# Attention with two heads on separate rows of TensorE, and a second staging buffer for the context's weights

## The chip, the cores and the metric

The kernel runs on one core of one Trainium2 chip. The metric is the device time of one execution in microseconds (us). TensorE (PE in the rows) multiplies and turns, VectorE is DVE, ScalarE is ACT, GpSimd is POOL, and SyncE (SP) issues the transfers. Each engine takes its own instructions strictly in order; semaphores order them against each other.

## The reference, cut to what matters

Two transformer blocks on 1024 tokens of width 1024, in fp32. The change touches the first block from its start up to the merge of the two attentions, and nothing of the feed-forward layers or of the second block.

```python
h  = modulate(rms_norm(x,   g1), sh1, sc1)     # 1024 tokens
hc = modulate(rms_norm(ctx, g1), csh1, csc1)   # 256 context tokens
q_a,k_a,v_a,q_b,k_b,v_b = split(h @ w_in)      # heads of 64; 8 query heads, 2 key heads in a
k_ac,v_ac,k_bc,v_bc     = split(hc @ w_in)     # the queries of the context are not needed
q, k = rms_norm per head; q_a, k_a = rope(...)
# A: blocks of 128 queries, keys of the block and its two neighbours, and the context
p = softmax([q_a k_a^T * 1/8 | band mask, q_a k_ac^T * 1/8, sink]);  o_a = p [v_a; v_ac]
# B: 128 queries (2 rows of a 16x64 grid), keys of 8 or 9 grid rows, and the context
p = softmax([q_b k_b^T * 1/8 + bias | mask, q_b k_bc^T * 1/8]);      o_b = p [v_b; v_bc]
x = x + g * concat(rms_norm(o_a), rms_norm(o_b)) @ w_out    # then SwiGLU, then block 2
```

## The kernel before, in words

A product of fp32 matrices is made of three products of the fast format fp32r: each operand is split into a high part and the rest (`w_hi`, `w_lo`, `ht_hi`, `ht_lo`), and high x high, high x rest and rest x high are added up.

**Context stage.** The 2 context tiles and then the 8 tiles of x are normed (`sum_tile` on ScalarE, `norm_tile` on GpSimd), scaled on VectorE (`scale_tile`, L278), shifted on GpSimd (`shift_tile`, L283), turned on TensorE (`turn_tile`, L293), and split on their way out of PSUM by ScalarE (`turned_hi`, L304) and VectorE (`turned_lo`, L308). Beside it go 5 panels of `w_in` (256 columns each) for the context: one buffer `stage` takes a panel, `split_hi` (ScalarE, L359) and `split_lo` (VectorE, L363) split it into one of two slots, and `load_weights` fetches the next panel when the split of the last is done. The loops of `pe_c`, `act_c`, `dve_c` and `pool_c` take one panel and one tile of x in each step: 5 steps with a panel, 3 with a tile alone. Then 9 panels for x follow, 8 tiles each.

**Keys.** Each of 10 token tiles holds 10 key heads. A key is split first (`key_hi`, `keys_dve`, L580), high part and rest side by side, then turned (100 turns), and copied to `kt`, so that a turned key head fills 128 rows: 64 of high parts, 64 of rests. `pool_q` does the same for each query tile of two heads, once as high|rest and once as rest|high; `pe_turn_q` turns these four.

**Attention.** A unit is one pair of heads (i = 0 to 3) and one block of 128 queries (n = 0 to 7); 32 units of phase A, then 32 of phase B. For each head j of the pair: scores (`pe_scores`, L744, two products on all 128 rows per piece of keys), mask and row minimum (`dve_min`, L925; the scores carry a minus), exponential and sum (`act_exp`, L841, L844, L846), turns of the probabilities (`pe_turn_p`, L754 the first four pieces, L761 the rest), copies to `prob_t` (`dve_p`, L932, 4 pieces; `act_p`, L857, the rest), products with the values of both heads on separate columns (`pe_values`, L775), and out (`dve_o`, `pe_turn_o`, L781, `dve_on`, L961). `act_v` copies the values of the pair to `v_pair` once per pair, and waits for all products of the last pair. In units with n = 0, 1, 6, 7 of phase B, which are called edge units here, `dve_min` and `act_exp` work in two steps each, the second step of the exponential reading the masked scores; the other units are joined. `dve_tables` makes the tables of bias of a pair. Between A and B everything runs empty, and then B's first queries are turned.

The order in a unit is written out by hand. TensorE's is

```python
pe_turn_p(n, 0); pe_scores(n+1, 0); pe_values(n-1); pe_turn_q(n+2)
pe_turn_p(n, 1); pe_scores(n+1, 1); pe_turn_o(n-1)
```

After attention all engines meet at a barrier; whatever comes after it is not touched, but for one instruction per tile in the merge.

## Time and profile before

| | |
|---|---|
| median of 3 runs | 2659.41 us (2658.87 to 2660.73) |
| the profiled execution's own time | 2660.4 us |
| its span | 2658.6 us |
| mean granted clock of TensorE | 0.965 |
| busy TensorE / VectorE / ScalarE / GpSimd | 92% / 61% / 40% / 13% of the span |
| 44.0 to 123.4 us | context stage |
| 123.4 to 361.6 us | 9 panels for x |
| 361.6 to 378.2 us | keys |
| 378.2 to 529.6 us | attention, phase A |
| 529.6 to 739.3 us | attention, phase B, and the barrier |
| 739.3 us to the end | merge, feed-forward, second block |

The span runs from the first to the last instruction; the execution's own time has 1.8 us around it. An engine's busy share says nothing of what limits a stage: a stage is as long as the chain of waits through it. The stretches are read from the first product of each stage, and the time between two equal instructions of neighbouring units is the period of the loop.

### The profile page before, as it was taken

The numbers are of one execution on the slowest core, as the hardware profiler recorded it, in microseconds if no ns is written. First come the engines' busy times: TensorE is split into PE (matmuls) and PEld (weight loads), VectorE is DVE, ScalarE is ACT, GpSimd is POOL, SyncE is SP. The second block draws the span as 40 slices with busy tenths as digits, with TensorE's granted clock in tenths as the row PEclk, the third lists the DMA queues.
The fourth block names the chain that finished last, engine by engine and source line by source line (L and its number), as shares of the span: only waits on it lengthen the run. The fifth ranks groups of instructions, "written<-read, shape, count | busy, mean of one in ns | idle before, by whom it ended". The sixth has DMA issues, their size and how long they took to land. (4 is left out here: it accounts for less than half of the span.)

```text
span 2658.6 us, 42198 instructions
## 1 busy us (share of the span) xinstructions
PE 2458.3 (92%) x15597; PEld 2118.0 (80%) x15597; DVE 1618.2 (61%) x2691; ACT 1064.3 (40%) x2111; POOL 358.6 (13%) x507
## 2 busy tenths in 40 slices
PE   4799989989869799999999999997897999999998
PEld 2788887778769688888888799995795888878886
DVE  3523347767755877777677932107538777667677
ACT  1422245555531432333254432224435454544444
POOL 2566312222111100000000010003212000000001
PEclk8899999999979899999999999997998999999999
DMA  8233320000042133233375431110231444377453
GB/s 290 92 115 113 124 54 1 1 2 1 1 151 80 64 104 103 91 119 103 109 263 184 141 116 48 39 36 3 75 109 64 156 155 148 135 254 252 135 186 115
DMA packets 189033, 288.15 MB, mean 108 GB/s; under 512 B 11704, under 2 KB 109948, under 8 KB 188540
## 3 DMA queue, kind: packets, MB, share of 16 engines
q1 hardware_dynamic: 188860, 285.84, 32.2%
q8 instruction: 109, 1.79, 0.3%
q14 instruction: 64, 0.52, 0.1%
HBM read 219.46 MB, written 67.34 MB: 108 GB/s over the span
## 5 line engine op out<-in xcount | busy, mean ns | idle before, releaser
L378 PE MATMUL ps<-w_hi,ht_hi 128*128 128x256 f32 x1744 | 504.0, 289 | 17.6 <-DVE w_lo L363 8.3
L379 PE MATMUL ps<-w_lo,ht_hi 128*128 128x256 f32 x1744 | 498.4, 286 | 0.0
L380 PE MATMUL ps<-w_hi,ht_lo 128*128 128x256 f32 x1744 | 498.0, 286 | 0.0
L378 PEld LDWEIGHTS ps<-w_hi,ht_hi 128*128 128x128 f32 x1744 | 338.1, 194 | 34.3 <-issue 11.3
L379 PEld LDWEIGHTS ps<-w_lo,ht_hi 128*128 128x128 f32 x1744 | 338.3, 194 | 0.0
L380 PEld LDWEIGHTS ps<-w_hi,ht_lo 128*128 128x128 f32 x1744 | 338.1, 194 | 0.0
L363 DVE TENSOR_TENSOR w_lo<-stage,w_hi 128x2048 fp32r<-128x2048 f32 x31 | 73.9, 2382 | 217.5 <-ACT w_hi L359 217.5
L1687 PE MATMUL ps<-ff_b_hi,ff_a_hi 128*128 128x512 f32 x448 | 174.6, 390 | 2.6 <-DVE ff_b_lo L1675 1.4
L1689 PE MATMUL ps<-ff_b_hi,ff_a_lo 128*128 128x512 f32 x448 | 174.3, 389 | 0.0
L1688 PE MATMUL ps<-ff_b_lo,ff_a_hi 128*128 128x512 f32 x448 | 174.3, 389 | 0.0
L1445 PE MATMUL ps<-ht_hi,swiglu_w_hi 128*128 128x512 f32 x352 | 138.2, 393 | 10.1 <-DVE tmp L1955 7.7
L1402 ACT ACTIVATE swiglu_w_hi<-swiglu_stage 128x512 fp32r<-128x512 f32 x110 | 69.0, 631 | 175.1 <-PE ps L1447 153.2
L1446 PE MATMUL ps<-ht_lo,swiglu_w_hi 128*128 128x512 f32 x352 | 137.6, 391 | 0.0
L1447 PE MATMUL ps<-ht_hi,swiglu_w_lo 128*128 128x512 f32 x352 | 137.5, 391 | 0.0
L1648 ACT ACTIVATE ff_a_hi<-ff_a_raw 128x512 fp32r<-128x512 f32 x112 | 70.8, 632 | 165.7 <-PE ps L1689 148.7
L1673 DVE TENSOR_TENSOR ff_a_lo<-ff_a_raw,ff_a_hi 128x512 fp32r<-128x512 f32 x112 | 77.5, 692 | 90.0 <-ACT ff_a_hi L1648 89.9
L1687 PE MATMUL ps<-swiglu_b_hi,swiglu_a_hi 128*128 128x512 f32 x308 | 120.5, 391 | 5.0 <-DVE swiglu_b_lo L1675 5.0
L1689 PE MATMUL ps<-swiglu_b_hi,swiglu_a_lo 128*128 128x512 f32 x308 | 119.9, 389 | 0.0
L1688 PE MATMUL ps<-swiglu_b_lo,swiglu_a_hi 128*128 128x512 f32 x308 | 119.9, 389 | 0.0
L775 PE MATMUL ps<-prob_t,v_pair 128*64 128x128 f32 (+1 forms) x1440 | 96.1, 279 | 23.9 <-ACT v_pair L869 9.0
L841 ACT ACTIVATE probs<-masked,small 128x641 f32<-128x641 f32 (+2 forms) x96 | 83.1, 866 | 83.6 <-DVE small L925 83.5
L744 PE MATMUL ps<-kt,q_t 128*128 (+3 forms) x640 | 115.8, 312 | 0.0
(362 smaller groups left out, 5731.7 us busy)
## 6 DMA issues: line engine op xcount, KB each, us to landing
ff_a_raw<-ff_act_dram SPq DMA_DIRECT2D x112, 256.0 KB, 2.8
stage<-w_in SPq DMA_DIRECT2D x23, 1024.0 KB, 5.2
swiglu_a_raw<-swiglu_act_dram SPq DMA_DIRECT2D x77, 256.0 KB, 3.2
stage<-w_mod SPq DMA_DIRECT2D x16, 1024.0 KB, 5.5
ff_stage<-w_ff SPq DMA_DIRECT2D x16, 1024.0 KB, 5.4
ff_act_dram<-ff_act_sums SPq DMA_DIRECT2D x16, 1024.0 KB, 4.3
ff_act_dram<-ff_acts SPq DMA_DIRECT2D x16, 768.0 KB, 5.7
swiglu_stage<-w_up SPq DMA_DIRECT2D x11, 1024.0 KB, 5.2
```

The costliest lines, as they stand in the source:

```text
L378: pe.matmul(bank, a, wh[:, k, :], start=(k == 0), stop=False)
L379: pe.matmul(bank, a, wl[:, k, :], start=False, stop=False)
L380: mm = pe.matmul(bank, b, wh[:, k, :], start=False, stop=(k == KT - 1))
L744: mm = pe.matmul(dst, q_t[:, n % 2, j, o, :], keys_of(ph, i, j, a, w), start=(o == 0), stop=(o == 1))
L775: mm = pe.matmul(ps[HD * j:HD * j + HD, 7, 0:P], v_pair[0:rows, tile, HD * j:HD * j + HD], prob_t[n % 2][0:rows, j, c * P:(c + 1) * P], st ...
L841: act.activation(probs_s[:, j, first:8 + CTX + width], masked_s[:, j, first:8 + CTX + width], ACT.Exp, bias=low, scale=-1.0, accum_out=den ...
L1445: pe.matmul(bank(q, b), w7_hi[b][:, k, :], x_of(0, b, k), start=(k == 0), stop=False)
L1446: pe.matmul(bank(q, b), w7_hi[b][:, k, :], x_of(1, b, k), start=False, stop=False)
L1447: mm = pe.matmul(bank(q, b), w7_lo[b][:, k, :], x_of(0, b, k), start=False, stop=(k == 3))
L1687: pe.matmul(bank, a_hi[r][:, cols], b_hi[r][:, :], start=first, stop=False)
L1688: pe.matmul(bank, a_hi[r][:, cols], b_lo[r][:, :], start=False, stop=False)
L1689: return pe.matmul(bank, a_lo[r][:, cols], b_hi[r][:, :], start=False, stop=last)
```

## The change

- Context: a second buffer `stage_2` takes the panels 1, 3 and 5, the first of them fetched in the middle of the tiles of x. VectorE shifts the two context tiles itself and makes the gain of x after them. All 8 tiles of x are spread over the 5 steps with a panel (`TURNS`), two in a step or one, and turned between the row tiles of a panel.
- Keys and queries are turned unsplit (50 turns for the keys, one per query block and pair, four at a time), and split when they leave PSUM: ScalarE takes the high part, VectorE the rest. `kt` holds two heads on 2 x 64 rows, high parts and rests apart. `k_split`, `q_split`, `v_pair`, `pool_q` and `act_v` are gone.
- Scores: three products per piece and head on 64 rows, the two heads in turn on rows 0 to 63 and 64 to 127. The head pairs of phase A are (i, i+4), one of each key head, for which the query columns are stored in another order, undone in the merge by one more instruction per tile.
- Scores of the next unit come first in a unit, both heads together; all pieces of a head's probabilities leave PSUM in one copy, head 0 by ScalarE, head 1 by VectorE. The first scores of B follow A's last unit without a break, and the tables are made in four parts.

The diff, with its core alone; the lines taken out are those of the functions printed above.

```diff
+    stage_2 = at("stage_2", [2048], F32, nat + NT * D * 4 + 10 * KVW * 4 + 12288)
...
+    kt = at("kt", [5, 2, S + CTX], F32R, ht)
...
         def load_weights(sp, p, source, dst=None):
+            if isinstance(p, int) and p in SECOND:
+                if p > 1:
+                    sp.wait_ge(w_lo_done, p - 1)
+                sp.dma_start(stage_2[:, :].rearrange("p (k n) -> p k n", k=KT), source).then_inc(w_landed_2, 16)
+                return
+            if isinstance(p, int) and p - 1 in SECOND:
+                sp.wait_ge(w_lo_done, p - 1)
+            elif not isinstance(p, int) or p > 0:
                 sp.wait_ge(w_lo_done, p)
             sp.dma_start(stage_up() if dst is None else dst, source).then_inc(w_landed, 16)
...
+        SECOND = (1, 3, 5)
...
         def keys_pe(pe):
+            pe_turn_q(pe, 0, 0, 0)
             pe.wait_ge(dense_evac, D_O)
+            pe.wait_ge(modx_row, 16)
             for j in range(10):
+                if j >= 3:
+                    pe.wait_ge(kt_lo, j - 2)
+                for h in range(5):
+                    col = A_KV + P * h if h < 4 else 0
+                    mm = pe.transpose(ps[:, 2 * (j % 3) + h // 4, (h % 4) * P:(h % 4 + 1) * P], k_nat[:, j, col:col + P], ident[:, :])
                 mm.then_inc(kt_tr, 1)
...
         def keys_act(act):
...
+            act.wait_ge(*panel_used(P_O - 1))
+            act_q(act, 0, 0, 0)
             for j in range(10):
                 act.wait_ge(kt_tr, j + 1)
...
+                act.activation(kt[:, :, 0, j * P:(j + 1) * P], turned_keys(j), ACT.Copy).then_inc(kt_hi, 1)
...
         def keys_dve(dve):
...
+            dve_q(dve, 0, 0, 0)
...
             for j in range(10):
...
+                dve.wait_ge(kt_hi, j + 1)
+                dve.tensor_tensor(kt[:, :, 1, j * P:(j + 1) * P], turned_keys(j), kt[:, :, 0, j * P:(j + 1) * P].bitcast(F32),
+                                  ALU.subtract).then_inc(kt_lo, 1)
...
+        TURNS = [(0, 1), (2, 3), (4,), (5,), (6, 7)]
...
+            for s, turns in enumerate(TURNS):
+                for j in turns:
+                    if j + 2 < NT:
+                        norm_tile(pool, j + 2, T_X, D)
+                        shift_tile(pool, j + 2, NC, shift_x)
...
         def pe_c(pe):
...
+            for s, turns in enumerate(TURNS):
+                for b in rows_pe(pe, s, s % 2, NC, T_C, NC * s, lag=2, at=C_AT):
+                    if b < len(turns):
+                        turn_tile(pe, turns[b], turns[b] % 2, T_X)
...
+            for s, turns in enumerate(TURNS):
+                split_hi(act, s + 1, (s + 1) % 2)
+                if s < 4:
+                    turn(turns[0])
+                heads_act(act, C_PANELS[s], None, NC, NT, NC * s, NC * s)
+                for j in turns[1 if s < 4 else 0:]:
+                    turn(j)
...
+            def turn(j):
+                turned_lo(dve, j, j % 2, T_X)
+                x_scaled(j + 2)
...
+            for s, turns in enumerate(TURNS):
+                if s < 4:
+                    turn(turns[0])
+                heads_dve(dve, C_PANELS[s], last, s + 1, NC, NT, NC * s, NC * s, n)
+                last, n = (C_PANELS[s], n + 1) if C_PANELS[s][0] != "v" else (None, n)
+                for j in turns[1 if s < 4 else 0:]:
+                    turn(j)
...
+            rows = slice(HD * j, HD * j + HD)
...
+                return kt[rows, 4, part, a:a + width]
+            if isinstance(i, int):
+                return kt[rows, i, part, a:a + width]
+            return kt[rows, ds(i, 1), part, a:a + width].squeeze(1)
...
...
+                pe.wait_ge(ql_done, g)
+            for b in range(4):
+                mm = pe.transpose(ps[:, 6, b * P:(b + 1) * P], pair_cols(ph, i, n + b), ident[:, :])
             mm.then_inc(qt_done, 1)
...
+        def pe_scores(pe, ph, i, n):
...
+            pe.wait_ge(ql_done, quad(ph, i, n) + 1)
+            if isinstance(u, int) and u == 0:
+                pe.wait_ge(kt_hi, 10)
+                pe.wait_ge(kt_lo, 10)
+            elif joined(*preceding(ph, i, n)[0::2]):
+                pe.wait_ge(min_done, 2 * u)
+            else:
+                pe.wait_ge(exp_done, 2 * u)
+            if ph == A:
+                parts = [(0, CTX, S, CTX), (1, 0, first * P, width)]
+            else:
+                parts = [(0, 0, S, CTX), (0, CTX, first * P, 256), (1, 0, first * P + 256, width - 256)]
+            for bank, at0, a, w in parts:
+                for m, (x, y) in enumerate(((0, 0), (0, 1), (1, 0))):
+                    for j in range(2):
+                        mm = pe.matmul(ps[:, 2 * j + bank, at0:at0 + w], q_t[HD * j:HD * j + HD, n // 4, x, (n % 4) * P:(n % 4 + 1) * P],
+                                       keys_of(ph, i, j, y, a, w), start=(m == 0), stop=(m == 2))
+            mm.then_inc(s_done, 1)
...
+            if j:
+                pe.wait_ge(pa_evac, u + 1)
+            elif not isinstance(u, int) or u > 0:
+                pe.wait_ge(pb_evac, u)
...
         def attention_pe(pe):
+            pe_scores(pe, A, 0, 0)
...
+                def pair(i, ph=ph):
                     for n in range(NB):
+                        ahead, behind = following(ph, i, n), preceding(ph, i, n)
+                        if ahead:
+                            pe_scores(pe, *ahead)
                         pe_turn_p(pe, ph, i, n, 0)
                         if behind:
+                            pe_values(pe, *behind)
+                        if n % 4 == 1 and next_quad(ph, i, n):
+                            pe_turn_q(pe, *next_quad(ph, i, n))
                         pe_turn_p(pe, ph, i, n, 1)
                         if behind:
...
+        def act_p(act, ph, i, n):
             u = unit(ph, i, n)
+            act.wait_ge(pt_done, 2 * u + 1)
             if not isinstance(u, int) or u > 1:
...
+            act.activation(prob_t[n % 2][:, 0, 0:cols], source, ACT.Copy).then_inc(pa_evac, 1)
...
                     for n in range(NB):
+                        ahead = following(ph, i, n)
+                        act_p(act, ph, i, n)
                         for j in range(2):
...
+                        if n % 4 == 1 and next_quad(ph, i, n):
+                            act_q(act, *next_quad(ph, i, n))
...
+        def dve_q(dve, ph, i, n):
+            dve.wait_ge(qh_done, quad(ph, i, n) + 1)
+            dve.tensor_tensor(q_t[:, n // 4, 1, :], ps[:, 6, :], q_t[:, n // 4, 0, :].bitcast(F32), ALU.subtract).then_inc(ql_done, 1)
...
+            dve.wait_ge(s_done, u + 1)
+            if not isinstance(u, int) or u > 0:
+                dve.wait_ge(exp_done, 2 * u - 1 + j)
...
+            dve.wait_ge(pt_done, 2 * u + 2)
...
+            dve.tensor_copy(prob_t[n % 2][:, 1, 0:cols], source).then_inc(pb_evac, 1)
...
+            dve.memset(inner[:, :, 0:CTX], 0.0)
...
+                        ahead, behind = following(ph, i, n), preceding(ph, i, n)
                         if ahead:
+                            dve_min(dve, *ahead, 0)
+                            dve_min(dve, *ahead, 1)
                         if behind:
...
+                            dve_o(dve, *behind)
                         dve_sums(dve, ph, i, n)
...
+                        dve_p(dve, ph, i, n)
+                        if n % 4 == 2 and next_quad(ph, i, n):
+                            dve_q(dve, *next_quad(ph, i, n))
                         if behind:
...
+                            dve_on(dve, *behind)
+                        if following(ph, i, NB - 1) and (ph == B or isinstance(i, int) and i == PAIRS - 1):
+                            heads = 0 if ph == A else i + 1
+                            if n == NB - 2:
+                                dve_edge(dve, heads, 0)
+                                dve_edge(dve, heads, 1)
+                            if n == NB - 1:
+                                dve_inner(dve, heads, 0)
+                        if ph == B and n == 0:
+                            dve_inner(dve, i, 1)
...
                 sp.dma_start(q_nat[:, j, :], t["x"][0, j * P:(j + 1) * P, :]).then_inc(x_in[j], 16)
+                if j == 3:
+                    load_weights(sp, 1, panel_of(t["w_in"], CTX_COLS[1]))
...
+            dve.wait_ge(mod_added, 16)
+            dve.scalar_tensor_tensor(out=gain_c, in0=gain_c, scalar=1.0, in1=norm1[:, :], op0=ALU.add, op1=ALU.mult).then_inc(mod_added, 1)
+            for j in range(NC):
+                if j == 0:
+                    dve.wait_ge(mod_added, 17)
+                scale_tile(dve, j, j, T_C, ctx_in[:, j, :], gain_c, True)
+                dve.wait_ge(xs_done, j + 1)
+                dve.tensor_tensor(xn[:, j, :], xn[:, j, :], shift_c, ALU.add).then_inc(xn_done, 1)
+            dve.scalar_tensor_tensor(out=gain_x, in0=gain_x, scalar=1.0, in1=norm1[:, :], op0=ALU.add, op1=ALU.mult).then_inc(mod_added, 1)
+            split_lo(dve, 0, 0)
+            for j in range(NC):
+                turned_lo(dve, j, j, T_C, at=C_AT)
...
+            dve_c(dve)
...
+                    source, gain, dst = row_tile(q_nat, j, g * AW, AW), on_ab[:, g * AW:(g + 1) * AW], xn[:, b, g * AW:(g + 1) * AW]
+                    if g == 1:
+                        last = dve.scalar_tensor_tensor(out=dst, in0=source, scalar=root, in1=gain, op0=ALU.mult, op1=ALU.mult)
+                        continue
+                    for kv in range(2):
+                        dve.scalar_tensor_tensor(out=dst[:, kv * PN:(kv + 1) * PN].rearrange("p (i d) -> p i d", d=HD),
+                                                 in0=source.rearrange("p (i j d) -> p i j d", j=2, d=HD)[:, :, kv, :], scalar=root,
+                                                 in1=gain[:, kv * PN:(kv + 1) * PN].rearrange("p (i d) -> p i d", d=HD),
+                                                 op0=ALU.mult, op1=ALU.mult)
```

TensorE in the middle of phase A, one unit from one turn of probabilities to the same turn of the next; L744 are scores, L775 values, L721 the query's turns. Before:

```order
913 L754 MATMUL ps<-ident,probs 128x128 x4
914 L761 MATMUL ps<-ident,probs 128x128
915 L744 MATMUL ps<-kt,q_t 128x256 x2
916 L744 MATMUL ps<-kt,q_t 128x384 x2
917 L775 MATMUL ps<-prob_t_90,v_pair 64x128 x10
918 L721 MATMUL ps<-ident,q_split 128x128 x4
919 L754 MATMUL ps<-ident,probs 128x128 x4
920 L761 MATMUL ps<-ident,probs 128x128
921 L744 MATMUL ps<-kt,q_t 128x256 x2
922 L744 MATMUL ps<-kt,q_t 128x384 x2
923 L781 MATMUL ps<-ident,o_t 128x128
```

The same place in the changed kernel; L769 are scores, L781 probabilities, L794 values, L800 the output's turn.

```order
946 L769 MATMUL ps<-kt,q_t 128x256 x6
947 L769 MATMUL ps<-kt,q_t 128x384 x6
948 L781 MATMUL ps<-ident,probs 128x128 x5
949 L794 MATMUL ps<-prob_t_91,v_nat 64x128 x10
950 L781 MATMUL ps<-ident,probs 128x128 x5
951 L800 MATMUL ps<-ident,o_t 128x128
```

The scores stand ahead of everything else in the unit, 12 products in place of 8; the query's four turns are left in two units of eight only.

VectorE in the context stage from the gain of the context to the second panel's split; L278 scales, L308 splits a turned tile, L363 a panel. Before:

```order
18 L1178 SCALAR_TENSOR_TENSOR mod_83<-mod_83,norm_84 128x1024 x2
19 L278 SCALAR_TENSOR_TENSOR xn<-ctx_in,rstd,mod_83 128x1024 x2
20 L308 TENSOR_TENSOR ht_lo<-ps,ht_hi 128x8x128 x2
21 L363 TENSOR_TENSOR w_lo<-stage,w_hi 128x2048
22 L1184 TENSOR_SCALAR head_gain<-head_gain 128x64 x2
23 L1185 TENSOR_SCALAR neg_sink<-neg_sink 128x8
24 L278 SCALAR_TENSOR_TENSOR xn<-q_nat,rstd,mod_83 128x1024
25 L363 TENSOR_TENSOR w_lo<-stage,w_hi 128x2048
```

In the changed kernel, where L294, L324 and L379 are the same three and L1154 is the shift:

```order
19 L294 SCALAR_TENSOR_TENSOR xn<-ctx_in,rstd,mod_84 128x1024
20 L1154 TENSOR_TENSOR xn<-xn,mod_84 128x1024
21 L294 SCALAR_TENSOR_TENSOR xn<-ctx_in,rstd,mod_84 128x1024
22 L1154 TENSOR_TENSOR xn<-xn,mod_84 128x1024
23 L1155 SCALAR_TENSOR_TENSOR mod_84<-mod_84,norm_85 128x1024
24 L379 TENSOR_TENSOR w_lo<-stage,w_hi 128x2048
25 L324 TENSOR_TENSOR ht_lo<-ps,ht_hi 128x8x128 x2
26 L294 SCALAR_TENSOR_TENSOR xn<-q_nat,rstd,mod_84 128x1024 x2
27 L324 TENSOR_TENSOR ht_lo<-ps,ht_hi 128x8x128
28 L294 SCALAR_TENSOR_TENSOR xn<-q_nat,rstd,mod_84 128x1024
29 L379 TENSOR_TENSOR w_lo<-stage_69,w_hi 128x2048
```

The split of the first panel moved ahead of the turned context tiles, and three tiles of x are scaled ahead of the second panel's split, where one was.

## Rows read from the trace of the kernel before

**Rows 1.** Stretches: engine busy us (count), PEclk granted clock, DMA share, GB/s.
```profile
44.00:123.40 79.40, 51.15 (x320) 47.81 (x321) 46.60 (x41) 33.27 (x49) 46.97 (x35) 0.73 0.38 129
123.40:361.60 238.20, 238.20 (x2018) 216.34 (x2016) 69.90 (x107) 60.13 (x147) 108.09 (x57) 1.00 0.32 106
361.60:378.20 16.60, 13.28 (x110) 11.68 (x109) 11.95 (x17) 13.54 (x29) 4.04 (x12) 1.00 0.33 81
378.20:529.60 151.40, 136.20 (x1326) 114.54 (x1324) 113.06 (x337) 87.53 (x217) 40.24 (x126) 1.00 0.05 9
529.60:739.30 209.70, 178.96 (x1788) 160.68 (x1788) 145.01 (x369) 118.69 (x292) 42.48 (x120) 0.96 0.01 1
```

**Rows 2.** Timeline of the context stage: start, us, engine, line, operation, idle before.
```profile
44.63 2.36 DVE L1178 SCALAR_TENSOR_TENSOR mod<-mod,norm 128x1024 f32<-128x1024 f32 x2
...
65.75 1.91 ACT L359 ACTIVATE w_hi<-stage 128x2048 fp32r<-128x2048 f32 x1 [6.32 <-DMA stage<-w_in]
67.70 2.29 DVE L363 TENSOR_TENSOR w_lo<-stage,w_hi 128x2048 fp32r<-128x2048 f32 x1 [5.37 <-ACT w_hi L359]
...
70.32 1.27 DVE L278 SCALAR_TENSOR_TENSOR xn<-q_nat,rstd,mod 128x1024 f32<-128x1024 f32 x1
72.07 1.23 DVE L308 TENSOR_TENSOR ht_lo<-ps,ht_hi 128x1024 fp32r<-128x1024 f32 x1 [0.47 <-ACT ht_hi L304]
...
96.56 3.80 DVE L363 TENSOR_TENSOR w_lo<-stage,w_hi 128x2048 fp32r<-128x2048 f32 x1 [3.49 <-ACT w_hi L359]
...
123.43 0.56 PE L378 MATMUL ps<-w_hi,ht_hi 128*128 128x256 f32 x1
```

**Rows 3.** The page's DMA issues: count, KB each, us from issue to landing.
```profile
stage<-w_in SPq DMA_DIRECT2D x23, 1024.0 KB, 5.2
```

**Rows 4.** Timeline of VectorE while the keys are turned.
```profile
366.44 0.81 DVE L580 TENSOR_TENSOR k_split<-k_nat,k_split 128x640 f32<-128x640 f32 x1
```

**Rows 5.** Timeline of TensorE, one phase-A unit.
```profile
441.83 1.31 PE L775 MATMUL ps<-prob_t,v_pair 128*64 128x128 f32 x20
443.08 0.66 PE L721 MATMUL ps<-ident,q_split 128*128 128x128 f32 x4
443.57 0.60 PE L754 MATMUL ps<-ident,probs 128*128 128x128 f32 x4
444.01 0.27 PE L761 MATMUL ps<-ident,probs 128*128 128x128 f32 x1
444.03 0.83 PE L744 MATMUL ps<-kt,q_t 128*128 x4
```

**Rows 6.** The same timeline, ScalarE and VectorE.
```profile
443.04 0.83 ACT L841 ACTIVATE probs<-masked,small 128x641 f32<-128x641 f32 x1 [0.59 <-DVE small L925]
...
444.21 0.69 DVE L932 COPY prob_t<-ps 128x512 f32<-128x512 f32 x1 [0.72 <-PE ps L754]
444.91 0.88 DVE L925 CUSTOM_DVE_ANT_0 masked<-ps,band,small 128x640 f32<-128x640 f32 x1
```

**Rows 7.** Timeline of VectorE, last row sum of A and first of B.
```profile
526.62 0.15 DVE L947 RECIPROCAL rden<-den 128x2 f32<-128x2 f32 x1
...
543.50 0.17 DVE L947 RECIPROCAL rden<-dsum 128x2 f32<-128x2 f32 x1
```

**Rows 8.** Groups by form in phase B: count | busy, mean ns | idle before.
```profile
L775 PE MATMUL ps<-prob_t,v_pair 128*64 128x128 f32 x768 | 50.0, 279 | 15.2 <-ACT v_pair L869 9.0 <-DVE q_nat L961 6.1
...
L920 DVE TENSOR_REDUCE small<-ps 128x1 f32<-128x256 f32 x32 | 13.4, 420 | 5.0 <-PE ps L744 4.9
...
L925 DVE CUSTOM_DVE_ANT_0 masked<-ps,edge,small 128x512 f32<-128x512 f32 x32 | 24.0, 751 | 4.1 <-issue 0.5
...
L844 ACT ACTIVATE probs<-ps,small 128x256 f32<-128x256 f32 x32 | 15.2, 475 | 44.2 <-DVE small L925 44.2
...
L846 ACT ACTIVATE probs<-masked,small 128x512 f32<-128x512 f32 x32 | 22.8, 711 | 0.0
...
L973 DVE SCALAR_TENSOR_TENSOR edge<-raw_bias,col_mask 128x896 f32<-128x896 f32 x8 | 8.4, 1090 | 0.0
```

414 lines of the change are left out of this document (125 added, 289 removed).

## The prediction, made blind

> **What bounds the kernel now.** I read the stretches first, with the granted clock [rows 1]; then the timelines of the four places that the change touches, on all engines; then the groups by form, for what a wait costs in total. The nine panels for x are TensorE's own: 238.20 us busy of 238.20, 2018 products, so 0.118 us for one of 256 columns. Nothing in the change touches that rate, so this stretch only moves, and so does everything behind the barrier. The other four stretches have air in them: TensorE is busy 51 of 79 us in the context stage, at a mean clock of 0.73; 13.3 of 16.6 at the keys; 136 of 151 in phase A and 179 of 210 in B. These 457 us are what can shrink. All sums are against the profiled execution's own 2660.4 us; the median of the runs shown is 1.0 below it, which I take off at the end.
>
> **Context stage.** The reader is to see one loop [rows 2, 3]: a panel lands 5.2 us after its issue, its high part takes ScalarE 1.91 and its rest VectorE 2.29, and only then is the next one fetched. So a step costs 9.4 us or more whatever it holds, five of them stand in a row, and three tiles of x are left behind them until the first product for x at 123.43. With the second buffer a panel is fetched one step earlier and its 5.2 us lie beside the step before. What is late next is VectorE's row of work. The start: gain of the context 1.18 (half of 2.36) from 44.63, two scalings at 1.27 and two shifts (1.2 each, an estimate by the scaling of the same size) done on VectorE itself, the gain of x 1.18, the first rest 2.29, two turned context tiles at 1.23: done at 56.7. A step with two tiles of x then holds one rest, two scalings, two turned rests and about 1.1 of head sums, 8.4 us, and around 1.6 of waiting for TensorE in between, 10 us. The step's first turned tile waits for its turn behind 24 products (2.8 us), and the panel's rest is queued behind it on VectorE, so TensorE's next panel waits for both. Second panel from 68.7, then 78.7, 88.7 and 98.7, the last two tiles turned at 107; first product for x at about 108, **-15.5 us**. From one side, VectorE's work alone adds up to 48 us behind 44.6, which would be -30. From the other, one of the rests took 3.80 in place of 2.29 while GpSimd worked beside it, and there is more such company now: four times 1.5 us leaves -9. The panel fetched in the middle of x's tiles delays tiles 4 to 7 and the small constants by up to 5 us; tile 4 is needed at about 71, the constants after 107. GpSimd loses two shifts and is not late.
>
> **Keys.** Before, 16.6 us from the last panel to the first score [rows 1]. Now a tile takes five turns (0.11 each, below), a high part of 640 columns on ScalarE and a rest of 640 columns on VectorE; the same work from SBUF took 0.81 [rows 4]. Ten rests in a row behind 0.5 of waiting, 0.55 of turns, 0.25 to their end and about 0.7 of high part are 10.1 us: **-6.5 us**, give or take 1.5. The first query's turn and split lie ahead of it. The gains and the rope are done well before.
>
> **Attention, phase A.** First the prices on TensorE [rows 5]. Turns of 128 columns step by 0.11 (four of them from 443.57 to 444.01). The 20 recorded value products end 1.31 after the first began; less one product's 0.27 that is 1.04, 0.055 each, half a turn's step: products for separate columns of the array ran two at a time. Leaving them costs 0.10 more than a step: the last began at 442.87, the next turn at 443.08. I take this 0.10 for each change of the array's shape. A score of 384 columns is 1.5 times 0.118, 0.177. By this rule an inner unit before is 8 scores 1.18, 10 turns 1.10, values 1.10, four turns of the query 0.44, output 0.11, two changes 0.20: 4.13 us, where 151.4 / 32 = 4.73 were needed; the rest is waiting.
> After: six pairs of scores 3 x (0.118 + 0.177) = 0.885 if the two heads run side by side on their rows, 1.10, 1.10, 0.11 for a quarter of a query's turns, 0.11, and four changes 0.40: 3.71. Units at the band's ends (two of eight) have 4 pieces: 3.09. Waits: the scores of n+1 stand at the head of TensorE's queue and need both minima of n; behind them stand the turns of n and the values of n-1, and ScalarE's copy waits for those turns. From the end of one unit's scores, VectorE needs 0.2 + 2 x 0.88 [rows 6] to the second minimum, 2.0 us, and TensorE comes for it after 2.8: met. VectorE's copy (640 columns, about 0.83 by the 0.69 for 512) ends some 0.1 before TensorE wants the place again: just met. So TensorE is the bound, with 0.15 per unit for such near misses: 6 x 3.71 + 2 x 3.09 + 1.2 = 29.6 per pair, 118.4 for four. ScalarE has two exponentials (0.83 and about 0.1), one copy and a quarter of a query, 2.9 of 3.7. What else goes: the copy of the values to `v_pair` and the wait for it, GpSimd's four operations per unit, which nothing waited for (0).
>
> **The seam and phase B.** From the last row sum of A to the first of B are 16.88 us [rows 7]; now one unit and the tables, about 7. In B a joined unit is scores 3 x (0.118 + 0.118 + 0.147) = 1.15, turns 1.54, values 1.54, 0.22, five changes 0.50: 4.95. The four edge units are a chain instead, since the next scores now wait for both exponentials: scores 1.06, change and turns 0.76, values and changes 1.52, turns 0.66, 0.27 to the end of the last, exponentials 1.19 [rows 8], a start of 0.1: 5.5. The minima (2 x (0.42 + 0.75)) lie beside it. One query in each pair stands in such a chain, 0.44, and VectorE's two tables of 1.09 stick out by about 1.5. Pair: 4 x 4.95 + 4 x 5.5 + 0.44 + 1.5 = 43.7. Before, the values alone waited 9.0 us for `v_pair` in B [rows 8].
> From the first score to the merge: 3.3 until the first turn, 118.4, 1.5 for B's first tables, 174.8 for B less 3.0 for what its last unit lacks, 5 for the end and the barrier: 300, against 151.4 + 209.7 = 361.1: **-61 us**.
>
> **Merge.** Eight more VectorE instructions, two of 256 columns for one of 512; 2 x 0.42 against 0.69 [rows 6, 8] is 0.15 each, half of it hidden: +0.6.
>
> Sum: 2660.4 - 15.5 - 6.5 - 61.1 + 0.6 = 2577.9, as a median **2577 us**.
>
> **What is not in the trace: two heads on separate rows.** No row shows two products on rows 0 to 63 and 64 to 127. Best end: as the columns do, a pair in the time of one product, taken above. Below nothing is excluded, since the columns to stream are the same. Worst end: one after the other, each paying the change of shape. I take the best end, since the value products are the nearest row: same array, two parts, alternating.
> The Trainium skill (TensorE: Matmul & The Clock Gate, LDWEIGHTS) says that a load of weights takes the time of its columns, however few rows it has. That speaks against the change, which makes 12 loads of 128 columns out of 8; by it a pair could be no faster than two loads. The same page (Part 3: Packing small matmuls) says that loads for different rows overlap, with which the sum stays. No run here shows either.
>
> **Rivals.**
> *Loads in a row.* A load of 128 columns and its turn step by 0.11; if the loads of both heads share one way in, a unit's scores take 12 x 0.11 = 1.32 (+0.44, at the band's ends +0.61), in B 18 x 0.11 = 1.98 (+0.83, edge units +0.92): 24 x 0.44 + 8 x 0.61 + 16 x 0.83 + 16 x 0.92 = 43.5 us, 2620. The value products don't tell: the loads of a pair there are 64 columns each, 128 together, and a pair steps by 0.11.
> *Heads in a row.* The scores take twice: 24 x 0.885 + 8 x 0.71 + 16 x 1.15 + 16 x 1.06 = 62 us, 2639.
> *The order eats it.* The two places that are only just met in A are missed: turns wait for VectorE's copy, its copy for the turns, and a unit takes 4.2 in place of 3.7 and half a microsecond more in B too: 64 x 0.5 = 32 us, 2609. For it: 0.6 of waiting per unit before.
> *Slower.* Each step from one group of rows to the other is a change of shape that empties the array: 12 x (0.148 + 0.10) = 2.97 for the scores of an inner unit (+2.1), 1.9 more at the band's ends, +2.95 and +2.86 in B: 24 x 2.09 + 8 x 1.9 + 16 x 2.95 + 16 x 2.86 = 158 us, 2735. It turns the sign from 82 / 64 = 1.3 us per unit on. Against it: value products alternate between columns without any such price.
>
> **Chances.** Forecast 0.60 (own range 2560 to 2592), the order 0.12, loads 0.14, heads 0.09, slower 0.05. The range 2556 to 2630 holds the first three and the bounds of the context. No change within 0.2% (5 us, what a measurement of this kernel can tell) would need two of these to meet by accident: 0.01. Faster 0.94, slower 0.05.
>
> **What would show it.** First product for x at 108 (99 to 114); 10 us from the last panel to the first score; two score products starting within 0.02 us and the next pair 0.118 or 0.177 later; period 3.7 in A and 4.95 and 5.5 in B; one unit at the seam. I am wrong if score products step by 0.11 or more within a pair, if TensorE stands before L781 or L769 for over 0.3 us in each unit of A, or if the panels' rests in the context come no closer than 11 us.

## The result: 36 us faster, less than half of what was forecast

The changed kernel takes 2624.16 us (median of 4, 2621.37 to 2627.89), the one before 2660.07 in the same session: a ratio of 0.9864 (95% interval 0.9852 to 0.9876). The forecast was 2577, so of 83 us there came 36. The range of 2556 to 2630 holds the time, but the reasons behind its middle did not hold, and the range had been drawn for other losses than those that came.

The profiled execution has a span of 2622.9 us. Its stretches, as in [rows 1] (first product for x, last panel, first score, first merge transfer as bounds):

```profile
44.00:118.00 74.00, 49.06 (x324) 46.57 (x322) 52.55 (x39) 32.72 (x49) 38.73 (x30) 0.82 0.40 137
118.00:355.40 237.40, 237.40 (x2017) 215.70 (x2018) 68.56 (x108) 58.38 (x145) 113.37 (x60) 1.00 0.33 106
355.40:365.80 10.40, 7.67 (x58) 5.71 (x56) 8.47 (x12) 8.79 (x13) 0.00 (x0) 1.00 0.22 61
365.79:699.47 333.68, 285.90 (x3244) 232.80 (x3244) 240.22 (x656) 183.02 (x400) 0.00 (x0) 0.98 0.04 7
```

The same last stretch of the kernel before:

```profile
378.17:739.31 361.14, 315.19 (x3115) 275.24 (x3113) 258.07 (x705) 206.23 (x508) 82.76 (x245) 0.98 0.02 4
```

| | before | after | change | forecast |
|---|---|---|---|---|
| first product for x | 123.43 | 117.97 | -5.5 | -15.5 |
| from there to the first score | 254.7 | 247.8 | -6.9 | -6.5 |
| first score to merge | 361.1 | 333.7 | -27.5 | -61 |
| merge to the end | 1919.3 | 1923.4 | +4.1 | +0.6 |

These are single profiled executions. Six of the kernels below hold the context stage of the changed kernel line by line, and their first product for x comes at 114.88 to 120.24; with the old context stage it comes at 123.43 and, in experiment 7, at 125.33. So the context's gain is 3 to 10 us, by which two executions are compared, and -5.5 is one such pair. Part of the spread is TensorE's clock: from the first product of the last panel to the first product for x are 9.32 us in the changed kernel, at a mean granted clock of 0.82, and 7.81 in experiment 5, at 1.00.

The reader is to see in the last two windows that TensorE's busy time fell by 29 us, and that it stands as long as before: 46 us then, 48 now. The waits have moved. They stand on the page, in front of the context's first products (L394) and of the scores (L769):

```profile
L394 PE MATMUL ps<-w_hi,ht_hi 128*128 128x256 f32 x1744 | 506.0, 290 | 28.6 <-DVE w_lo L379 17.2
L769 PE MATMUL ps<-kt,q_t 64*128 64x256 f32 (+2 forms) x960 | 81.1, 307 | 40.6 <-DVE q_t L886 22.6
```

L886 (`dve_q`) makes the rest of the queries; most of what is left of the 40.6 us are B's edge units, whose scores wait for exponentials (14.0 us). The timeline around one such wait, in phase A:

```profile
414.48 0.58 ACT L837 ACTIVATE q_t<-ps 128x512 fp32r<-128x512 f32 x1
...
416.60 0.53 PEld L781 LDWEIGHTS ps<-ident,probs 128*128 128x128 f32 x5 [0.17 <-issue]
...
417.41 0.82 DVE L929 COPY prob_t<-ps 128x640 f32<-128x640 f32 x1 [0.32 <-PE ps L781]
...
418.15 0.68 DVE L886 TENSOR_TENSOR q_t<-ps,q_t 128x512 fp32r<-128x512 f32 x1
...
418.89 1.15 PE L769 MATMUL ps<-kt,q_t 64*128 64x256 f32 x12 [1.40 <-DVE q_t L886]
```

The high part was ready at 415.1. Its rest stands on VectorE behind the copy L929 of the unit, which waits for turns that TensorE has just done; TensorE comes to the next quad's scores at once, and waits for copy and rest: 1.40 us, and 1.67 in B, at one unit in four (a new quad, four blocks of queries turned together). A clean unit beside it takes 3.82 us from row sum to row sum (3.86 forecast), the one with the wait 5.29.

In the context the loop has the same shape. VectorE and GpSimd, and TensorE's first product of a panel:

```profile
58.70 2.37 POOL L299 TENSOR_TENSOR xn<-xn,mod 128x1024 f32<-128x1024 f32 x1
58.76 3.39 DVE L294 SCALAR_TENSOR_TENSOR xn<-q_nat,rstd,mod 128x1024 f32<-128x1024 f32 x1 [0.43 <-POOL rstd L279]
...
65.58 1.28 DVE L294 SCALAR_TENSOR_TENSOR xn<-q_nat,rstd,mod 128x1024 f32<-128x1024 f32 x1 [0.93 <-POOL rstd L279]
...
66.79 2.28 DVE L379 TENSOR_TENSOR w_lo<-stage,w_hi 128x2048 fp32r<-128x2048 f32 x1
66.95 4.39 POOL L299 TENSOR_TENSOR xn<-xn,mod 128x1024 f32<-128x1024 f32 x1 [1.40 <-DVE xn L294]
...
69.13 0.39 PE L394 MATMUL ps<-w_hi,ht_hi 128*128 128x256 f32 x1 [3.10 <-DVE w_lo L379]
...
96.33 0.58 PE L394 MATMUL ps<-w_hi,ht_hi 128*128 128x256 f32 x1 [6.24 <-DVE w_lo L379]
```

The panel's high part was ready at 58.8. Its rest L379 comes 8 us later, behind a scaling that waits for a root from GpSimd. And GpSimd's shift L299 takes 2.37 us where it comes first, and 4.39 where that rest has begun before it.

### The profile page after: what moved, and what is told of

It is laid out like the page before. It is cut to its first block and busy times, and to the rows that moved or that the text cites. A ratio compares the mean times of both kernels' runs of the same rounds, so it can differ in the third digit from the quotient of the medians.

```text
span 2622.9 us, 41034 instructions
## 1 busy us (share of the span) xinstructions
PE 2426.6 (93%) x15675; PEld 2075.1 (79%) x15675; DVE 1601.9 (61%) x2643; ACT 1033.2 (39%) x1983; POOL 268.3 (10%) x249
## 5 line engine op out<-in xcount | busy, mean ns | idle before, releaser
L394 PE MATMUL ps<-w_hi,ht_hi 128*128 128x256 f32 x1744 | 506.0, 290 | 28.6 <-DVE w_lo L379 17.2
L394 PEld LDWEIGHTS ps<-w_hi,ht_hi 128*128 128x128 f32 x1744 | 339.4, 195 | 45.5 <-DVE w_lo L379 18.5
L379 DVE TENSOR_TENSOR w_lo<-stage,w_hi 128x2048 fp32r<-128x2048 f32 x31 | 71.4, 2303 | 197.8 <-ACT w_hi L375 197.8
L275 POOL TENSOR_SCALAR msq<-sumsq 128x1 f32<-128x1 f32 (+1 forms) x26 | 8.1, 310 | 1088.8 <-ACT junk L287 703.4
L769 PE MATMUL ps<-kt,q_t 64*128 64x256 f32 (+2 forms) x960 | 81.1, 307 | 40.6 <-DVE q_t L886 22.6
L1423 PE MATMUL ps<-ht_hi,ff_w_hi 128*128 128x512 f32 x256 | 101.0, 395 | 10.7 <-DVE ht_lo L1324 8.9
```

Source lines behind the costliest of these rows:

```text
L379: dve.tensor_tensor(w_lo[:, slot, :], staged(p)[:, :], w_hi[:, slot, :].bitcast(F32), ALU.subtract).then_inc(w_lo_done, 1)
L394: pe.matmul(bank, a, wh[:, k, :], start=(k == 0), stop=False)
L769: mm = pe.matmul(ps[:, 2 * j + bank, at0:at0 + w], q_t[HD * j:HD * j + HD, n // 4, x, (n % 4) * P:(n % 4 + 1) * P], keys_of(ph, i, j, y, a ...
L1423: pe.matmul(bank(q, b), w7_hi[b][:, k, :], x_of(0, b, k), start=(k == 0), stop=False)
```

## The experiments

Each ratio is against the kernel before in the same session; "attention" is from the first score to the merge, in the profiled run. With the attention of the changed kernel unaltered it took 333.7 to 337.5 us (the changed kernel and experiments 8, 9 and 10), which is how closely these can be compared.

**1. The query's rest ahead of the copy** (`k1`) and **2. the high part between the exponentials as well** (`k7`).

```diff
                         dve_sums(dve, ph, i, n)
+                        if n % 4 == 2 and next_quad(ph, i, n):
+                            dve_q(dve, *next_quad(ph, i, n))
                         dve_p(dve, ph, i, n)
-                        if n % 4 == 2 and next_quad(ph, i, n):
-                            dve_q(dve, *next_quad(ph, i, n))
# k7 also, in attention_act:
                         for j in range(2):
                             if ahead:
                                 act_exp(act, *ahead, j)
-                        if n % 4 == 1 and next_quad(ph, i, n):
-                            act_q(act, *next_quad(ph, i, n))
+                            if j == 0 and n % 4 == 1 and next_quad(ph, i, n):
+                                act_q(act, *next_quad(ph, i, n))
```

> The changed kernel with one move on VectorE: in the third unit of each quad the query's rest stands ahead of the unit's copy of the turned probabilities, where it stood behind it. Theory 1 (the score products of the next quad stand at the head of TensorE's queue and wait for this rest): in the trace of the changed kernel they stood 1.40 us in A and 1.67 in B, 16 places, 22.6 us in all. The rest takes 0.68 and fills 0.32 us in which VectorE waited for the turns, so the copy comes 0.36 later; the wait falls from 1.4 to about 0.4 and the units' periods of 5.29 and 5.44 go to about 4.4: 13 to 18 us faster, 2607 to 2611. Theory 2 (VectorE's row of work sets these units, whatever the order): the copy is later by what the scores gain, and the time stays at 2624.

> As the first kernel of this call, and ScalarE's high part of the query stands between the two exponentials of its unit instead of behind both. Theory 1: this high part was ready 3.1 us before VectorE took its rest, so it is not late, and moving it changes nothing beside the first kernel; in phase A it falls into 0.7 us in which ScalarE waits for turns (0 to -2 us), in B's edge units, where the exponentials free the banks of the next scores, it costs up to 0.58 for each of 8 places (+2 to +5). Theory 2 (the high part on ScalarE is what is late): the time falls by 5 us or more beside the first kernel.

Measured: 2612.27 (ratio 0.9817, 0.9802 to 0.9831), attention 321.4, the unit of 5.29 now 4.19; and 2614.39 (0.9811, 0.9796 to 0.9825), attention 321.3. The wait was the rest's place on VectorE; where ScalarE makes the high part makes no difference that these runs can tell. The times lie a little above the 2607 to 2611 that were expected.

**3. Both halves where their engines are idle** (`k2`): the high part as in `k7`, and `dve_q` at the end of the unit with n % 4 == 1, behind `dve_on`.

> The changed kernel with both halves of the query's split moved to where their engines stand idle: ScalarE's high part between its two exponentials, VectorE's rest at the end of the quad's second unit, behind the scaling of the output, one unit earlier than in the changed kernel. Theory 1 (the next quad's scores waited for the rest; what was left with the rest ahead of the copy, 0.37 us per place, is the later copy of the probabilities): the minima that now come 0.4 us later have slack of 0.7, the units before a new quad go from 5.29 (4.19 with the first remedy) to 3.8 or 3.9 in A and from 6.86 (5.26) to 5.1 in B, first score to merge 313 to 317 us where it was 333.7 and 321.4: 17 to 20 us faster than the changed kernel, 2604 to 2608. Theory 2 (any place on VectorE costs the same 0.4, VectorE being as full as TensorE in these units): 321 us and 2611 to 2614 again.

Measured: 2608.64 (0.9792, 0.9775 to 0.9808), attention 316.9, units before a new quad 3.80 in A and 5.12 in B. So the wait had cost 333.7 - 316.9 = 16.8 us (15.7 to 20.5 over all pairs of runs with these two attentions); the remaining 0.37 per place was the late copy. The page had 22.6 us of waiting for the rest: 5 of them turned into waiting for B's exponentials, which went from 14.0 to 19.0. The window of this kernel, TensorE busy in the second place:

```profile
368.07:685.00 316.93, 287.43 (x3244) 234.88 (x3244) 238.84 (x656) 185.16 (x400) 0.00 (x0) 0.97 0.04 8
```

The work is that of the changed kernel; the waiting fell from 48 to 29.5 us.

**4. The second head on the first one's rows** (`s10`).

```diff
-  q_t[HD * j:HD * j + HD, n // 4, x, ...], keys_of(ph, i, j, y, a, w)
+  q_t[0:HD, n // 4, x, ...],               keys_of(ph, i, 0, y, a, w)
```

> The changed kernel, in which the score products of the second head read rows 0 to 63 too (it computes the first head's scores twice; the second head's are left out). As many instructions, columns and waits. Theory 1 (separate rows let two products run at once): with one group of rows they stand in a row, 0.885 us more per unit of A, 0.71 at the band's ends, 1.15 and 1.06 in B; TensorE is the bound in A, so a clean unit goes from 3.82 to 4.7: first score to merge +62 us, 2675 to 2690. Theory 2 (the pairs only start together in the records, and the array was never shared): clean units stay at 3.8 and the time at 2621 to 2628.

Measured: 2720.17 (1.0207, 1.0184 to 1.0231). The twelve score products of an inner unit of A, in this kernel and then in the changed one:

```profile
442.84 2.05 PE L769 MATMUL ps<-kt,q_t 64*128 64x256 f32 x12
```

```profile
422.70 1.15 PE L769 MATMUL ps<-kt,q_t 64*128 64x256 f32 x12
```

0.90 more, where the rows of before gave 0.885, and the clean unit went from 3.82 to 4.70. There no two products start together: they step by 0.117 to 0.121, and by 0.174 to 0.185 with 384 columns. Separate rows do run two products in the time of one. The time came out 30 us above the range of Theory 1. Beyond its 62 us there are 55 more in the window of the profiled run:

```profile
363.02:813.50 450.48, 403.58 (x3244) 342.92 (x3244) 241.46 (x656) 182.67 (x400) 0.00 (x0) 0.85 0.03 5
```

The mean granted clock fell to 0.85, with TensorE busier than before (90% of the stretch against 86%). This profiled run took 2737.18 us, 17 above the median of the five, at a mean clock over the span of 0.945 where the others had 0.950 to 0.953; so at the median some 38 of the 55 us are left. Which property of the work lowers the clock is not settled, nor how much of the 55 us is the clock's.

**5. Head by head** (`k5`): `for j` outside, `for m` inside in the score loop.

> The changed kernel with one loop turned: the three score products of the first head stand ahead of the three of the second, so that neighbours in TensorE's queue are on the same rows of the array and only one pair of six overlaps. Theory 1 (two heads run at once on separate rows, which is what halves the scores): a part of two pairs lost of three costs 2 x 0.118 or 0.177: 0.6 us per inner unit of A, 0.5 at the ends, 0.77 in B: 24 x 0.6 + 8 x 0.5 + 32 x 0.75 = 42 us if TensorE is the bound everywhere, less a part in the edge units and where scores wait: 25 to 42 us slower than the changed kernel, 2650 to 2666. Theory 2 (the two heads' products only start together in the records; the array takes them one after the other anyway): no change, 2621 to 2628.

Measured: 2630.5 (0.9879, 0.9860 to 0.9897), its interval meets that of the changed kernel; clean units 3.83. Theory 2 gave the right number, but experiment 4 refutes its reason. The start times in the trace suggest why: 419.681 and 419.691, 419.905 and 419.917, 420.021 and 420.038. Products still start in pairs, and the twelve take 1.15 us as in the changed kernel, where twelve on one group of rows took 2.05. So the pairs should be of the two heads, although three of one head stand ahead of three of the other in the program. That is inferred: a record names neither its rows nor its head.

**6. The order undone** (`k6`) and **7. the order alone, in the kernel before** (`s11`).

```diff
# k6, the changed kernel; s11 does the reverse in the kernel before, for both heads
+                        pe_turn_p(pe, ph, i, n, 0)
                         if ahead:
                             pe_scores(pe, *ahead)
-                        pe_turn_p(pe, ph, i, n, 0)
# s11 also: dve_min of both heads ahead of the unit's dve_p; in joined units
+                    pe.wait_ge(min_done, 2 * u - 1 + j)     # was exp_done
```

> The changed kernel with one part of the order undone: the next unit's scores stand behind the turns of the first head's probabilities, as before, and no longer at the head of the unit. Theory 1 (in A TensorE is busy throughout a clean unit of 3.82 us, so that its order is worth nothing there; at the 16 places where the scores wait for the query's rest, the turns of 0.77 us fill the wait): clean units stay at 3.8, the places with a wait go from 5.29 to 4.5 or 4.6; in B's edge units the scores come 0.8 later and the chain through the exponentials pays for it in 16 units: -12 + 8, so 2615 to 2628. Theory 2 (scores first is what keeps VectorE and ScalarE fed): clean units of A go to 4.4 or more as before the change, and the time rises by 20 us or more, 2644 and up.

> The kernel before with the new order alone: both heads' next scores at the head of TensorE's unit, VectorE's minima ahead of its copies, and in joined units the scores wait for the minimum and not for the exponential. Operands, turns of the query by units, copies and the context stay as before. Theory 1 (the order is what makes TensorE the bound, in either form of the products): by the rows of before an inner unit of A holds 4.13 us of TensorE's work, so its period goes from 4.47 to about 4.3, the waits for v_pair and for VectorE's four short copies stay: 5 to 12 us faster than before, 2648 to 2655. Theory 2 (the order helps only with the joined copies; here VectorE's copy of 512 columns after both minima comes late for TensorE's next turn, as one bank of probabilities is turned at a time): units grow to 4.7 to 5.0, 2670 to 2690. Scores ahead of turns was worth 36 us in the changed kernel; if it were worth as much here by itself, 2625.

Measured: `k6` 2660.94 (0.9993, 0.9983 to 1.0002), clean units of A 4.76; `s11` 2660.44 (0.9992, 0.9981 to 1.0002), units of 4.5 to 4.65. The two windows, `k6` and then `s11`:

```profile
362.75:732.63 369.88, 295.28 (x3244) 235.72 (x3244) 234.47 (x656) 187.47 (x400) 0.00 (x0) 0.98 0.03 6
```

```profile
380.09:741.04 360.95, 323.12 (x3115) 278.99 (x3113) 258.79 (x705) 207.15 (x508) 80.63 (x245) 0.98 0.02 5
```

| attention, us (TensorE busy) | old order | new order |
|---|---|---|
| old operands and copies | 361.1 (315) | 361.0 (323) |
| new operands and copies | 369.9 (295) | 333.7 (286) |

Neither half, as built here, is worth anything alone. The table is not a clean split: `k6` moves back the scores on TensorE alone and keeps VectorE's and ScalarE's new order, and the seam belongs to the operands' row. From the last but one row sum of A to the first of B are 19.9 us before and 20.5 in `s11`, but 13.7 in `k6` and 12.4 in the changed kernel, so that some 7.5 of the 27.5 us are the seam's. `k6` came out as its Theory 2 had it; in `s11` neither theory's time came. In `k6` TensorE's busy time stays low (295) and it stands 75 us. In `s11` the waiting fell from 46 to 38 us, but the recorded busy time of as many products rose by 8; why is open. The old form left an order nothing to win within a unit: over nearly four inner units of A, TensorE was busy throughout, in the kernel before and then in `s11`:

```profile
391.00:408.00 17.00, 16.78 (x168) 14.04 (x166) 13.30 (x37) 10.63 (x28) 4.67 (x15) 1.00 0.01 2
391.00:408.00 17.00, 16.87 (x166) 14.52 (x164) 13.62 (x35) 10.60 (x28) 4.98 (x16) 1.00 0.01 3
```

In `k6` the page has the wait that came in place of the work saved, a loop of scores, minimum, exponential and turn:

```profile
L781 PE MATMUL ps<-ident,probs 128*128 128x128 f32 (+1 forms) x720 | 106.2, 283 | 55.8 <-ACT probs L848 30.6
```

In `s11` TensorE hardly stands in a unit of A: at 436.70 only 0.19 us for a query's copy, between instructions in a row:

```profile
436.13 0.27 PE L765 MATMUL ps<-ident,probs 128*128 128x128 f32 x1
436.24 0.27 PE L785 MATMUL ps<-ident,o_t 128*128 128x128 f32 x1
436.70 1.43 PE L748 MATMUL ps<-kt,q_t 128*128 x8 [0.19 <-ACT q_t L825]
437.97 0.60 PE L758 MATMUL ps<-ident,probs 128*128 128x128 f32 x4
```

**8. One staging buffer** (`k4`): `SECOND = ()`, and the second panel fetched behind the small constants.

> The changed kernel with the second staging buffer undone: all panels of the context go through the first one, and the second panel is fetched behind the small constants, as before. Theory 1 (the steps of 13 us are set by VectorE and GpSimd, the transfer of 5.2 us lies beside them): the second panel comes late once, the others are hidden, and the first product for x is later by 0 to 4 us, 2624 to 2628. Theory 2 (the second buffer is what gave the 5.5 us, and without it the old loop of transfer, high part and rest of 9.4 us stands in a row with the tiles): 123 to 130 for that product and 2630 to 2636.

Measured: 2632.45 (0.9884, 0.9867 to 0.9900), first product for x at 123.26. That is the 123.43 of before, and 3.0 to 8.4 us later than in the seven profiled runs with the changed kernel's context stage (114.88 to 120.24); the time is about 5 us longer, though the intervals of the two ratios just meet. So by these runs the buffer and the early fetch gave most or all of the stage's gain. Whether the spread of the tiles over the steps gives anything by itself is not shown: no run has the buffer without it.

**9. The panel's rest first** (`k3`) and **10. x shifted on VectorE too** (`k8`).

```diff
# k3, dve_c
             for s, turns in enumerate(TURNS):
+                split_lo(dve, s + 1, (s + 1) % 2)
                 if s < 4:
                     turn(turns[0])
-                heads_dve(dve, C_PANELS[s], last, s + 1, NC, ...)
+                heads_dve(dve, C_PANELS[s], last, None, NC, ...)
# k8 also, x_scaled; shift_tile is gone from pool_c
                     scale_tile(dve, j, j % 2, T_X, q_nat[:, j, :], gain_x, True)
+                    shift_tile(dve, j, NC, shift_x)
```

> The changed kernel with one move in the context stage: VectorE takes the rest of the next weight panel at the start of each step, ahead of the turned tile and of the scaling of the tile two further on. Theory 1 (the rest was late because it stood behind a scaling that waited for GpSimd's root): the first product of the panels now starts after w_lo at gaps of 3.1, 4.7, 6.2 and 3.0 us, 17 us in all; most of that goes, steps come down from 13.0 to 10 to 11, first product for x at 108 to 110 instead of 118: 7 to 10 us faster, 2614 to 2617. Theory 2 (GpSimd's row of work is the bound: shifts of 2.4 us that take 4.35 beside VectorE's rests, roots and norms, about 11 to 12 us per two tiles): the gaps move from the rests to the turned tiles, the first product for x comes at 115 to 118, and the time stays at 2621 to 2624.

> The kernel with the panel's rest first (first product for x at 112.0), and in addition the shift of x's tiles is done by VectorE behind its scaling and no more by GpSimd. Theory 1 (GpSimd's row bounds the stage: a shift takes it 2.4 us, and 4.35 when a panel's rest runs on VectorE beside it; VectorE then waits 1.4 to 4.1 us for each root): VectorE takes 8 x 1.23 = 9.8 us more, its waits of about 17 us for roots fall to 3, and VectorE works without gaps: first product for x at 103 to 107, 5 to 9 us less than with the rest first alone. Theory 2 (GpSimd's delays lie beside other waits, TensorE's clock and panels): VectorE only gets 9.8 us more to do and the first product for x comes at 112 to 118.

Measured: first product for x at 112.02 and at 101.30; 2617.99 (0.9825, 0.9811 to 0.9838) and 2608.55 (0.9789, 0.9772 to 0.9807). With the rest first the product comes 6.0 us earlier than in the changed kernel and 2.9 to 8.2 earlier than in all runs with its context, a bit less than expected; the time's interval lies clear below. What is late then is GpSimd: VectorE waits 14.9 us for its roots. In `k8` the stage lost 10.7 us more although VectorE does 9.8 us more work; experiments 11 and 12, with the same context, have the product at 99.76 and 100.23. Groups by form in that stage, `k3` and then `k8`:

```profile
L299 POOL TENSOR_TENSOR xn<-xn,mod 128x1024 f32<-128x1024 f32 x8 | 25.9, 3233 | 9.6 <-DVE xn L294 9.6
L379 DVE TENSOR_TENSOR w_lo<-stage,w_hi 128x2048 fp32r<-128x2048 f32 x6 | 17.4, 2898 | 0.0
L294 DVE SCALAR_TENSOR_TENSOR xn<-q_nat,rstd,mod 128x1024 f32<-128x1024 f32 x8 | 12.4, 1547 | 14.9 <-POOL rstd L279 14.9
```

```profile
L379 DVE TENSOR_TENSOR w_lo<-stage,w_hi 128x2048 fp32r<-128x2048 f32 x6 | 13.7, 2283 | 0.0
L294 DVE SCALAR_TENSOR_TENSOR xn<-q_nat,rstd,mod 128x1024 f32<-128x1024 f32 x8 | 10.2, 1276 | 1.6 <-POOL rstd L279 1.6
L299 DVE TENSOR_TENSOR xn<-xn,mod 128x1024 f32<-128x1024 f32 x8 | 9.8, 1225 | 0.3
```

A shift takes VectorE 1.23 and GpSimd 3.23 on the mean; VectorE's rests and scalings are shorter without GpSimd beside them (2.28 for 2.90, 1.28 for 1.55), and its waits for roots fell from 14.9 to 1.6. The Trainium skill (SBUF — State Buffer, SBUF: two separate sides) says that VectorE with two SBUF inputs and GpSimd hold a shared pair of ports in turn, each for its whole instruction. The trace agrees: the shift of 4.39 us that is recorded from 66.95 on is one of 2.37 behind what was left of VectorE's rest, which ended at 69.07, and VectorE's scaling of 3.39 from 58.76 on is one of 1.27 behind the shift that ended at 61.07.

**11. Experiments 3 and 10 together** (`s9`), and **12. phase B's tables on GpSimd** (`s12`): `dve_edge` and `dve_inner` called from GpSimd's stream, the edge table as one subtraction.

> The early split of the query and both edits of the context (panel's rest first, shift of x on VectorE) together. Theory 1 (the two losses lie in stages that don't overlap): they add up. First product for x at 101.3 and first score to merge 316.9 us, 16.7 and 16.8 below the changed kernel: 2592, within 2588 to 2596. Theory 2 (what is gained ahead is given back later, by TensorE's clock or the transfers): 2597 to 2606.

> As the first kernel of this call, and phase B's bias tables are made by GpSimd, not by VectorE. Theory 1 (the tables stand in VectorE's row ahead of minima that TensorE's next scores wait for; GpSimd is idle then): of 3.6 us of VectorE per pair, 1.0 to 1.5 stood out: the pair's last period of 6.3 and the seam of 7.5 go down by 1 to 2 us each: 4 to 8 us faster than the first kernel, 2585 to 2589. Theory 2 (as in the context, a GpSimd operation on long rows and VectorE's operations from and to SBUF stretch each other, and the table of 896 columns takes GpSimd over 2 us, so that the next minima wait longer): 0 to 8 us slower, 2592 to 2600.

Measured: 2590.28 (0.9727, 0.9714 to 0.9741) and 2591.08 (0.9732, 0.9719 to 0.9746). The gains add up, and `s9` beats both kernels, by 72 us and by about 36. Its context and attention:

```profile
44.00:99.80 55.80, 44.58 (x321) 42.94 (x321) 52.88 (x47) 32.65 (x49) 19.44 (x22) 0.85 0.53 180
347.59:665.55 317.96, 288.37 (x3244) 235.75 (x3244) 239.09 (x656) 184.99 (x400) 0.00 (x0) 0.97 0.04 8
```

VectorE is busy 52.88 of 55.80 us in the context, so there is next to nothing left to win there without taking work from it. The place of the tables makes no difference. On GpSimd the two of a pair take 3.82 us, and VectorE's next minimum waits for them:

```profile
521.21 3.82 POOL L972 TENSOR_TENSOR edge<-col_mask,raw_bias 128x896 f32<-128x896 f32 x2 [40.73 <-DVE small L925]
525.17 0.42 DVE L920 TENSOR_REDUCE small<-ps 128x1 f32<-128x256 f32 x1 [2.02 <-POOL edge L972]
```

On VectorE they take 2.1 us. But in both kernels, in the pair looked at, the tables are ready almost as soon as the scores that this minimum reads: it starts 1.70 us after the first of its score products in `s12` and 1.81 in `s9`, where one unit later, with no edge table in front, it is 1.58 and 1.57. So the tables stick out by 0.1 to 0.2 us, and the rest of the period is the chain through scores, minima and exponentials. The pair's last period stayed at 6.4 to 6.5, the seam's at 7.47.

## Why the prediction was right or wrong

- **Keys**, -6.5 forecast: from the end of the last panel to the first score 16.5 us became 10.2, -6.3; the other 0.6 of the table's -6.9 lie in the panels for x. Right, and the prices with it: ten rests took 8.08 us for 8.1, the first high part 0.70 for 0.7.
- **Two heads on separate rows**, best end: right, shown by experiment 4. The trace has the two products of a pair 0.003 to 0.010 us apart and the next pair 0.11 to 0.118 or 0.166 to 0.175 later. The rivals "loads in a row", "heads in a row" and "slower" fall. That a pair could be no faster than two loads, as the prediction had worked out against its own sum, did not hold: one load and its turn step by 0.11, and a pair with its two loads by 0.11 to 0.118. The Trainium skill (TensorE: Matmul & The Clock Gate, Part 3: Packing small matmuls) says that a load of weights overlaps with products in flight only when it is for other rows. The trace agrees as far as it shows: the two loads of a pair start 0.003 us apart, and on one group of rows (experiment 4) they step by 0.108 or more.
- **"TensorE is the bound" in A**: a clean unit was 3.82 for 3.86. But this holds at 6 units of 8. The step that failed in attention is the query's. I counted `dve_q` and `act_q` as busy time (0.17 us per unit, 0.11 of turns) and didn't ask what the scores at the head of TensorE's queue wait for at a new quad. The prediction named that queue's head and checked it against the minima alone. Measured: 16.8 us. The rival "the order eats it" named the right kind of loss, with other places: turns and copies that just meet did meet. Its argument, 0.6 us of waiting per unit before, was a misreading: 4.73 is a mean with the pairs' first units of 6.0 us in it. An inner unit took 4.47, with TensorE busy 16.78 of 17.00 us, so the 4.13 counted for it was too little and what was missing was not waiting. That 3.82 lies so close to 3.86 is in part luck: the 3.86 held 0.11 for a quarter of a query's turns and 0.15 for near misses, and a clean unit has neither. Without them it was priced 3.60. The 0.22 more are the changes of shape, counted at 0.10 each. In the unit from 456.69 to 460.51 each of the four cost 0.09, and 0.05 to 0.10 more before the second product or pair (the second pair of scores starts 0.22 behind the first, where 0.118 was counted).
- **The rest of attention.** Without that wait, 316.9 us stand against 300. Units at a band's end took 3.6 for 3.24 and those in which a query is turned 4.1 to 4.2 for 3.86, together 1.3 us per pair of A: 5. B's full pairs took 44.7 to 45.5 for 43.7, mostly in the edge units, whose chain was priced 5.5 us and took 5.6 to 7.4: 5. That a pair's tables stick out by 1.5 us was wrong the other way (0.2 in experiment 11). The start took 5.2 us for 3.3 until the first turn, and the first pair 2.4 more than the others. About 2 are left for the seam.
- **The start, and the clock.** From 368.2 to 378.4 us the granted clock was at 0.5, which is 1.2 GHz; before, it stayed at 1.0 there. Ahead of it TensorE had been busy 7.67 us of 10.4 at the keys, where it was 13.28 of 16.6 [rows 1], and then stood 1.74 and 2.29 us around the first scores. The second unit's scores took 1.97 us for 1.15. Every run with the new form shows such a stretch there, and neither run with the old one does; what in the work brings it is not shown.

```profile
368.20:378.40 10.20, 8.56 (x51) 6.68 (x53) 4.88 (x12) 4.97 (x11) 0.00 (x0) 0.50 0.71 132
```

- **Context**, -15.5 forecast, -5.5 came (3 to 10 over all profiled runs). The failed step is "GpSimd loses two shifts and is not late". I took VectorE's row of work as what is late, 10 us per step, and gave GpSimd's company a price of four times 1.5 us on VectorE. It is the other way round: GpSimd's roots and its stretched shifts hold VectorE, and the panel's rest is queued behind a wait for them. Steps took 13.0, 12.8, 14.4 and 12.3 us, over the 11 that the prediction had named as a sign of being wrong. Experiments 9 and 10 show both parts: with both mended the product stands at 101.3, ahead of the forecast's 108.
- **Merge**: +0.6 forecast, and next to nothing came. For 770 us behind the merge's first transfer nearly all instructions stand within 0.25 us of their old places. The +4.1 come behind that, in work that the change doesn't touch, beside a mean clock of 0.93 for 0.94. Over the kernels here that part varies from 1919.3 to 1926.0 us. Why is open.

## What to carry to other kernels

Where an engine's queue has one instruction at its head that everything stands behind, list each semaphore that it waits for, at each turn of the loop, and not only the usual one: a piece of work that is cheap and rare costs its whole delay there. Here work taken from an engine showed only with the new order, and the order only with less work: price such changes together. A stage that is read from one execution can be off by several microseconds, so put an effect of that size beside other runs of the same code. Before a transfer is hidden, look at which helper engine the stage's busiest one waits for, and how long their operations take side by side.

## What the hardware did that I had not expected

- Products started in pairs, 0.010 to 0.017 us apart, though in the program three of one head came before three of the other. That the pairs are of different rows is inferred from their time. The order among heads cost nothing that shows in a unit (3.83 against 3.82 us).
- With the scores on one group of rows, the granted clock fell to a mean of 0.85 over attention, from 0.98, although TensorE was busier.
- GpSimd's shift of 1024 columns took 2.37 to 4.39 us, VectorE's 1.23, and moving eight of them to the busier engine shortened the stage by 10.7 us.
